# The per-layer gate of a decoder step computed with seven half-size products per pair of token tiles

## The chip, the core and the metric

One Trainium2 chip, one of its cores. TensorE multiplies, VectorE and ScalarE work on rows of SBUF and PSUM, GpSimd issues the gathers and SyncE most of the other transfers. The metric is the device time of one execution in microseconds; lower is better. The kernel before ran three times: 830.54, 834.19 and 836.55 us, with a median of 834.19.

## What is computed

The reference is one layer of a hybrid decoder (retention, gated DeltaNet, a mixture of experts, a per-layer input embedding) over 576 tokens of 1024 numbers, all float32. The change touches the last stage, behind the experts:

```python
h = h + moe
u = rmsnorm(h, norm_ple)
gate = jax.nn.sigmoid(jnp.einsum('bld,de->ble', u, w_ple_gate))   # 1024 x 1024 weights
h = h + gate * jnp.einsum('blp,pd->bld', p_l, w_ple_proj)
# and then the final RMSNorm, which is stored
```

## The kernel before, in words

The 576 tokens lie in five tiles: tiles 0 to 3 have 128 rows, tile 4 has 64. `LAST` is the order in which the last stage takes them (0, 1, 4, 2, 3); k below is a place in that order. Each engine has its own instruction stream, written out by hand in one function per engine, and each runs its stream strictly in the order written. Semaphores tie them together; a wait holds everything behind it on that engine.

The experts run in 12 phases of 128 rows (`down`, L1296). The rows of a phase go from PSUM to `yb` (ScalarE, `y_evac`) and from there to `y_slots` in HBM. GpSimd waits until all phases are stored, then gathers two rows for each token (`ga`, L2706): the first two tiles at once, each later tile when VectorE has used up the buffers of an earlier one.

For each tile, then:
- VectorE `combine` (L2428): two scaled additions of the gathered rows to the residual `h2`; `h3` counts them.
- ScalarE squares the row and takes the root (L1745, L1748), VectorE inverts it (`r3`, L2444).
- TensorE `u3_transpose` (L1398): eight transposes of 128 columns into two PSUM banks; VectorE `u3_evac` (L2438) multiplies by the norm's gain into `u3T`.
- TensorE gate (L1414): for each half of 512 output columns, eight matmuls over the 1024 input columns, in one PSUM bank. The 64-row tile puts its two column quarters side by side on the array (`sides`).
- ScalarE sigmoid (L1759) with the row's factor as its scale, VectorE `gated` (L2451, L2452) times `pp` and plus `h2`; `h4` counts the halves.
- ScalarE squares each half (L1765) and takes the root (`ms_root`, L1769), VectorE `mean0` (L2462) and `finish` (L2470, L2475), and SyncE stores the tile. The last tile is stored in two halves, one scaled by VectorE, one by ScalarE.

`pp`, the product of `p` and `w_proj`, is computed ahead of the gate (`p_product`, L1384): that of tile 0 earlier, those of tiles 1 to 3 before the first transposes, that of tile 4 after them. Sigmoid and Sqrt need different tables on ScalarE; a change of table is an ACT_TABLE_LOAD. `link` marks an instruction of VectorE or ScalarE that the next one must wait for.

The gate's weights are two tiles of 512 output columns, `w_pg[0]` and `w_pg[1]`, 2 MB each, asked for by SyncE at L748 and L750, during the last two phases of the experts. The stored overflow slots (`ov_...`) are a small extra phase.

## Time and profile before

| | us |
|---|---|
| median of three runs | 834.19 |
| the profiled execution's own time | 832.21 |
| span of its instructions | 830.4 |
| busy: TensorE / VectorE / ScalarE / GpSimd | 810.4 / 385.0 / 214.2 / 151.0 |

The span runs from the first instruction to the last; 1.8 us of the execution's own time lie around it. A busy share is an average over stages with different limits: TensorE is busy for 98% of the whole span, and what the change is worth is read from the last 90 us.

### The profile page before, as it was taken

What the parts mean: (1) busy time and instruction counts of PE and PEld (TensorE: products, weight loads), DVE (VectorE), ACT (ScalarE), POOL (GpSimd) and SP (SyncE); (2) the same over time, 40 slices, a digit from 0 to 9 for tenths busy, and PEclk for the clock granted to TensorE, in tenths of its full rate; (3) what the DMA queues carried; (4) which work ended last, traced back from release to release, by engine and by line L of the source; (5) the groups of instructions that cost most, each with busy time, mean ns of one, the idle gap of its engine ahead of it and who ended that gap; (6) DMA issues with size and microseconds to landing.
All of it is one profiled execution on the core that took longest, in us unless ns stands there. A gap on an engine that the chain in (4) does not pass through costs nothing. (4 is left out here: it accounts for less than half of the span.)

```text
span 830.4 us, 12851 instructions
## 1 busy us (share of the span) xinstructions
PE 810.4 (98%) x5194; PEld 509.7 (61%) x5194; DVE 385.0 (46%) x859; ACT 214.2 (26%) x463; POOL 151.0 (18%) x182
## 2 busy tenths in 40 slices
PE   9999999999999999999999999999999999998996
PEld 4545777887889987777777776456343333344452
DVE  3223457584666523664853558636341111106443
ACT  3211152339324311121101101122121111124554
POOL 0234321004055224200220043000100001004000
PEclk9999999999999999999999999999999999999999
DMA  9520354403020200522252024036899999987111
GB/s 359 206 101 9 124 181 152 134 39 109 2 103 3 84 20 13 202 80 94 101 203 87 16 101 176 9 127 252 307 367 399 425 420 415 410 313 221 57 39 51
DMA packets 20896, 135.23 MB, mean 163 GB/s; under 512 B 2420, under 2 KB 3060, under 8 KB 13668
## 3 DMA queue, kind: packets, MB, share of 16 engines
q1 hardware_dynamic: 13392, 103.34, 31.9%
q0 software_dynamic: 4720, 23.83, 8.0%
...
## 5 line engine op out<-in xcount | busy, mean ns | idle before, releaser
L791 PE MATMUL pair<-mem 128*128 128x288 f32 x640 | 158.9, 408 | 0.0
L791 PEld LDWEIGHTS pair<-mem 128*128 128x128 f32 x640 | 120.5, 190 | 35.4 <-ACT mem L1435 2.1
L961 PE MATMUL single<-mem 128*128 128x288 f32 x448 | 110.1, 407 | 0.2
L961 PEld LDWEIGHTS single<-mem 128*128 128x128 f32 x448 | 84.8, 190 | 25.6 <-issue 1.6
L1346 PE MATMUL single<-mem 128*32 128x512 f32 x768 | 85.1, 594 | 0.9 <-DVE mem L2382 0.9
L1435 ACT ACTIVATE mem<-single 128x256 f32<-128x256 f32 (+5 forms) x109 | 44.6, 419 | 126.8 <-PE single L1209 48.5
L1435 ACT ACTIVATE mem<-pair 128x512 f32<-128x512 f32 (+5 forms) x78 | 33.5, 480 | 165.2 <-PE pair L791 63.1
L1414 PE MATMUL pair<-mem 128*128 128x512 f32 (+1 forms) x192 | 63.3, 524 | 0.0
L1346 PEld LDWEIGHTS single<-mem 128*32 128x32 f32 x768 | 23.7, 110 | 52.7 <-issue 51.6
L2375 DVE SCALAR_TENSOR_TENSOR mem<-single,mem 128x256 f32<-128x256 f32 x12 | 5.8, 484 | 102.3 <-PE single L1346 91.1
L1200 PE MATMUL pair<-mem 128*128 128x512 f32 x112 | 51.0, 601 | 0.0
L1414 PEld LDWEIGHTS pair<-mem 128*128 128x128 f32 (+1 forms) x192 | 28.4, 172 | 32.0 <-issue 29.5
L2094 DVE TENSOR_TENSOR mem<-mem,single 128x288 f32<-128x288 f32 x40 | 18.1, 452 | 55.7 <-PE single L961 52.2
L1296 PE MATMUL pair<-mem 128*32 128x512 f32 x384 | 43.7, 595 | 0.0
L1200 PEld LDWEIGHTS pair<-mem 128*128 128x128 f32 x112 | 20.4, 190 | 21.7 <-issue 21.4
L856 PE MATMUL pair<-mem 128*128 128x512 f32 (+1 forms) x96 | 32.1, 526 | 0.0
L2676 POOL DMA_INDIRECT mem<-u_rows,ids x12 | 11.4, 947 | 110.6 <-PE single L1281 100.5
L982 PE MATMUL pair<-mem 128*128 128x288 f32 x112 | 28.4, 409 | 0.2
L832 PE MATMUL pair<-mem 128*128 128x512 f32 x64 | 28.2, 596 | 0.4 <-DVE mem L1806 0.4
L1892 DVE SCALAR_TENSOR_TENSOR mem<-mem,vec 128x512 f32<-128x512 f32 x36 | 27.9, 774 | 1.3
L982 PE MATMUL single<-mem 128*128 128x288 f32 x112 | 27.8, 406 | 0.0
L1296 PEld LDWEIGHTS pair<-mem 128*32 128x32 f32 x384 | 11.3, 110 | 23.1 <-issue 23.0
...
## 6 DMA issues: line engine op xcount, KB each, us to landing
...
y_slots<-mem SPq DMA_DIRECT2D x9, 512.0 KB, 11.2
y_slots<-in_zeros POOLq DMA_DIRECT2D x8, 512.0 KB, 8.5
...
```

Of the source, the lines that this page charges most:

```text
L791: last = nc.tensor.matmul(pb[:, hf, 0:HALF], w(k), rhs[:, k, hf * HALF:(hf + 1) * HALF], start=(k == 0), stop=(k == kk - 1))
L832: last = nc.tensor.matmul(q_bank[t][rows, cols], uT[:, k, t * P:t * P + ntok(t)], ring[0][:, 512 * k + cols.start:512 * k + cols.stop], st ...
L856: last = nc.tensor.matmul(pair[plan.buf[s]][rows, 0, cols], uT[:, k, t * P:t * P + ntok(t)], w[:, k, cols], start=(k == 0), stop=(k == KD ...
L961: last = nc.tensor.matmul(single[plan.buf[s]][:, 0:HALF], lhs[:, k, :], rhs[:, k, :], start=(k == 0 and j in (0, 1, 3, 4)), stop=(k == 3), ...
L982: last = nc.tensor.matmul(fast_bank(s), lhs[:, k, :], rhs[:, k, :], start=(k == 0 and j in (0, 1, 3, 4)), stop=(k == 1), skip_group_check= ...
L1200: last = nc.tensor.matmul(sx_bank[j], rows[:, u, v, :], wgt[:, u, 512 * v:512 * v + 512], start=(i == 0 and j < 5), stop=(i == 3), skip_gr ...
L1296: last = nc.tensor.matmul(pair[p % 2][BS * g:BS * g + BS, n, :], hT[p % 2][:, k, BS * g:BS * g + BS], w_dn[e % 4][:, k, n * 512:(n + 1) * ...
L1346: last = nc.tensor.matmul(single[3][BS * g:BS * g + BS, :], xT[p % 2][:, k, BS * g:BS * g + BS], w_gu[e % 4][:, k, :], start=(k == 0), sto ...
L1414: last = nc.tensor.matmul(pair[(k + 1) % 2][rows, hf, cols], u3T[:, c, t * P:t * P + n], w_pg[hf][:, c, cols], start=(c == 0), stop=(c == ...
L1435: copy = lambda out, in_, scale=1.0: nc.scalar.activation(out, in_, ACT.Copy, scale=scale)
L1892: V.scalar_tensor_tensor(out=acc[m % 2][:, 0:LP], in0=cbuf[m % 2][:, j:j + LP], scalar=conv_w[:, m, j:j + 1], in1=acc[m % 2][:, 0:LP], op0 ...
L2094: V.tensor_tensor(to, plus, single[plan.buf[s]][:, 0:HALF], ALU.add).then_inc(ev(k0), 1)
```

## The change

For a pair of full tiles (0 and 1, then 2 and 3) the gate is a product of 256 x 1024 and 1024 x 1024, cut into 2 x 2 blocks on each side. Before, TensorE computed its eight block products. Now it computes seven, `p1, p2, p5, u2, p3, p4, p7` (L1430), each of four matmuls of 128 x 128 by 128 x 512, on sums and differences of blocks: `t1` to `t4` of the weights (128 x 2048 each, once) and `s1` to `s4` of the transposed rows (128 x 512 each, per pair). VectorE computes all of these. ScalarE copies four results per pair out of PSUM (`keep`), and VectorE adds them to others (`out`, four per pair) before the sigmoid, which now reads SBUF. `LAST` becomes 0, 1, 2, 3, 4, so that the 64-row tile comes last; it keeps its old product (L1466). `pg_sum`, `SUM_AT`, `KEPT` and the like number the sums, copies, squares and roots for the waits.

Besides: `w_pg[1]` is asked for in two halves of 1 MB, the second one only when all expert rows are stored. The last phase's second half is copied by VectorE instead of ScalarE, and one small overflow transpose moves into the middle of that phase. `p_product` of tile 4 moves ahead of the first transposes. The second `combine` step of tile 0 is cut into two halves, so that its first four transposes can begin after the first.

```diff
@@ tables @@
-LAST = [0, 1, 4, 2, 3]
+LAST = [0, 1, 2, 3, 4]
+PG_SUMS = [("t1", 0), ("s1", 0), ("t2", 0), ("s2", 0), ("c11", 0), ("s4", 0), ("s3", 0), ("t4", 0), ("t3", 0), ("c12", 0), ("c21", 0), ("c22", 0),
+   ("s1", 1), ("s2", 1), ("c11", 1), ("s4", 1), ("s3", 1), ("c12", 1), ("c21", 1), ("c22", 1), ("gain", 0), ("gain", 1)]
+SUM_AT = {s: i + 1 for i, s in enumerate(PG_SUMS)}
+PG_ORDER = ["p1", "p2", "p5", "u2", "p3", "p4", "p7"]
+KEPT = {(name, q): 6 + 4 * q + i for q in range(2) for i, name in enumerate(["p1", "p5", "u2", "p4"])}
...
+pg_t1, pg_t2, pg_t4 = (view(at, 4, 512) for at in (OR, BLK + 6144, UT))
+pg_t3 = [view(at, 2, 512) for at in (RINGO + 6144, UT + 3 * D)]
+pg_s1, pg_s2, pg_s4 = ([view(at, 4, P) for at in ats] for ats in
+                       ((RINGO + 4608, BLK + 17408), (RINGO + 5120, BLK + 17920), (RINGO + 5632, RINGO + 8192)))
...
+pg_bank = [(pair[1][:, 0, :], pair[1][:, 1, :], pair[0][:, 0, :]), (pair[0][:, 1, :], pair[1][:, 1, :], pair[0][:, 0, :])]
@@ SyncE @@
-    sp.dma_start(w_pg[1], a["w_pg1"].rearrange("k p c -> p k c")).then_inc(sem("w_pg"), 16)
+    sp.dma_start(w_pg[1][:, 0:4, :], a["w_pg1"][0:4].rearrange("k p c -> p k c")).then_inc(sem("w_pg"), 16)
...
-    sp.wait_ge(sem("h3"), 1)
+    sp.wait_ge(sem("y_stored0"), 16 * ((NPH + 1) // 2))
+    sp.wait_ge(sem("y_stored1"), 16 * (NPH // 2))
     sp.wait_ge(sem("w_pg"), 32)
+    sp.dma_start(w_pg[1][:, 4:8, :], a["w_pg1"][4:8].rearrange("k p c -> p k c")).then_inc(sem("w_pg"), 16)
+    sp.wait_ge(sem("h3"), 2)
+    sp.wait_ge(sem("w_pg"), 48)
@@ TensorE @@
+            if p == NPH - 1 and n == 0:
+                ov_hT(0)
...
-        pe.wait_ge(sem("h3"), k + 1)
+        pe.wait_ge(sem("h3"), k + 2 if k else 1)
         if k >= 2:
             pe.wait_ge(sem("u3T"), 2 * k - 2)
         for c in range(KD):
+            if k == 0 and c == 4:
+                pe.wait_ge(sem("h3"), 2)
             out = single[2 * (k % 2) + c // 4][:, (c % 4) * n:(c % 4 + 1) * n]
             last = nc.tensor.transpose(out, h2[0:n, t, c * P:(c + 1) * P], C("ident")[0:n, 0:n])
         last.then_inc(sem("u3_mm"), 1)
+    p_product(NT - 1)
     u3_transpose(0)
-    p_product(NT - 1)
-    for k, t in enumerate(LAST):
-        n = ntok(t)
-        pe.wait_ge(sem("u3T"), 2 * k + 2)
+    def gate_part(bank, rows, weights, start):
+        for c in range(4):
+            last = nc.tensor.matmul(bank, rows(c), weights(c), start=(start and c == 0), stop=(c == 3), skip_group_check=True)
+        return last
+    for q in range(2):
+        bank_a, bank_b, bank_c = pg_bank[q]
+        first, second = (lambda c: u3T[:, c, 2 * q * P:2 * q * P + P]), (lambda c: u3T[:, c, 2 * q * P + P:2 * q * P + 2 * P])
+        pe.wait_ge(sem("u3T"), 4 * q + 1)
         pe.wait_ge(sem("w_pg"), 32)
...
+        pe.wait_ge(sem("pp"), 4 + q)
+        gate_part(bank_a, first, lambda c: w_pg[0][:, c, :], True).then_inc(sem("pg_mm"), 1)
+        u3_transpose(2 * q + 1)
+        pe.wait_ge(sem("u3T"), 4 * q + 2)
+        if q:
+            pe.wait_ge(sem("pp"), KEPT["p4", 0])
+        gate_part(bank_b, lambda c: first(c + 4), lambda c: w_pg[0][:, c + 4, :], True).then_inc(sem("pg_mm"), 1)
+        pe.wait_ge(sem("pp"), 5)
+        pe.wait_ge(sem("pg_sum"), SUM_AT["s1", q])
+        gate_part(bank_c, lambda c: pg_s1[q][:, c, :], lambda c: pg_t1[:, c, :], True).then_inc(sem("pg_mm"), 1)
+        pe.wait_ge(sem("pp"), KEPT["p1", q])
+        pe.wait_ge(sem("pg_sum"), max(SUM_AT["t2", 0], SUM_AT["s2", q]))
+        gate_part(bank_a, lambda c: pg_s2[q][:, c, :], lambda c: pg_t2[:, c, :], False).then_inc(sem("pg_mm"), 1)
+        u3_transpose(2 * q + 2)
+        pe.wait_ge(sem("pp"), KEPT["p5", q])
+        pe.wait_ge(sem("pg_sum"), SUM_AT["s4", q])
+        gate_part(bank_c, lambda c: pg_s4[q][:, c, :], lambda c: w_pg[1][:, c + 4, :], False).then_inc(sem("pg_mm"), 1)
+        pe.wait_ge(sem("pg_sum"), max(SUM_AT["t4", 0], SUM_AT["c11", q]))
+        gate_part(bank_b, lambda c: second(c + 4), lambda c: pg_t4[:, c, :], True).then_inc(sem("pg_mm"), 1)
+        pe.wait_ge(sem("pp"), KEPT["u2", q])
+        pe.wait_ge(sem("pg_sum"), max(SUM_AT["t3", 0], SUM_AT["s3", q]))
+        gate_part(bank_a, second, lambda c: pg_t3[c // 2][:, c % 2, :], False).then_inc(sem("pg_mm"), 1)
+    pe.wait_ge(sem("u3T"), 2 * NT)
+    for hf in range(2):
+        if hf:
+            pe.wait_ge(sem("pp"), KEPT["p4", 1])
+        for c in range(KD):
+            for rows, cols in sides(4):
+                last = nc.tensor.matmul(pair[1][rows, hf, cols], u3T[:, c, 4 * P:TOK], w_pg[hf][:, c, cols],
+                                        start=(c == 0), stop=(c == KD - 1))
+        last.then_inc(sem("pg_mm"), 1)
@@ ScalarE @@
-        copy(yb[b][:, 512:D], pair[b][:, 1, :]).then_inc(sem("y_ready"), 1)
+        if e_done < NPH:
+            copy(yb[b][:, 512:D], pair[b][:, 1, :]).then_inc(sem("y_ready"), 1)
...
+    def gate(k, hf):
+        t, n = LAST[k], ntok(LAST[k])
         act.wait_ge(sem("r3"), k + 1)
+        if k < 4:
+            act.wait_ge(sem("pg_sum"), SUM_AT[("c11", "c12", "c21", "c22")[2 * (k % 2) + hf], k // 2])
+            half = sgp[k % 2][:, 512 * hf:512 * hf + 512]
+            last = nc.scalar.activation(half, half, ACT.Sigmoid, scale=ms[:, 2, t:t + 1])
+        else:
+            act.wait_ge(sem("pg_mm"), 15 + hf)
+            act.wait_ge(sem("h4"), 5 + hf)
             for rows, cols in sides(t):
+                last = nc.scalar.activation(sgp[0][0:n, 512 * hf + cols.start:512 * hf + cols.stop], pair[1][rows, hf, cols],
                                             ACT.Sigmoid, scale=ms[0:n, 2, t:t + 1])
+        last.then_inc(sem("sgp"), 1)
...
+    def keep(name, q):
+        act.wait_ge(sem("pg_mm"), 7 * q + PG_ORDER.index(name) + 1)
+        k, hf, bank = {"p1": (0, 0, 0), "u2": (0, 1, 0), "p4": (1, 0, 1), "p5": (1, 1, 2)}[name]
+        if q:
+            act.wait_ge(sem("h4"), 2 * k + hf + 1)
+        copy(sgp[k][:, 512 * hf:512 * hf + 512], pg_bank[q][bank]).then_inc(sem("pp"), 1)
+    row_root(0)
+    row_root(1)
+    keep("p1", 0)
+    gate(0, 0)
+    keep("p5", 0)
+    half_square(0, 0)
+    keep("u2", 0)
+    row_root(2)
+    gate(0, 1)
+    keep("p4", 0)
+    half_square(0, 1)
+    last_root(0)
...
+    half_square(2, 1)
+    last_root(2)
+    keep("p4", 1)
+    gate(3, 0)
+    half_square(3, 0)
+    gate(3, 1)
+    link(nc.scalar.activation(hT[0][0:1, 0, 0:1], C("eps", 1), ACT.Sqrt))
+    half_square(3, 1)
+    last_root(3)
+    gate(4, 0)
+    half_square(4, 0)
+    gate(4, 1)
+    link(nc.scalar.activation(hT[0][0:1, 0, 0:1], C("eps", 1), ACT.Sqrt))
+    half_square(4, 1)
+    last_root(4)
@@ VectorE @@
+    dve.wait_ge(sem("dn_mm"), NPH)
+    dve.wait_ge(sem("y_stored1"), 16 * ((NPH - 1) // 2))
+    V.tensor_copy(yb[1][:, 512:D], pair[1][:, 1, :]).then_inc(sem("y_ready"), 1)
...
+    w11, w12, w22 = w_pg[0][:, 0:4, :], w_pg[1][:, 0:4, :], w_pg[1][:, 4:8, :]
+    def weights_1():
+        dve.wait_ge(sem("w_pg"), 32)
+        V.tensor_tensor(pg_t1, w12, w11, ALU.subtract).then_inc(sem("pg_sum"), 1)
+    def weights_2():
+        dve.wait_ge(sem("w_pg"), 48)
+        dve.wait_ge(sem("pg_sum"), SUM_AT["t1", 0])
+        V.tensor_tensor(pg_t2, w22, pg_t1, ALU.subtract).then_inc(sem("pg_sum"), 1)
+    def weights_4():
+        dve.wait_ge(sem("pg_sum"), SUM_AT["t2", 0])
+        V.tensor_tensor(pg_t4, w_pg[0][:, 4:8, :], pg_t2, ALU.subtract).then_inc(sem("pg_sum"), 1)
+    def weights_3():
+        dve.wait_ge(sem("pp"), 5)
+        V.tensor_tensor(pg_t3[0], w22[:, 0:2, :], w12[:, 0:2, :], ALU.subtract)
+        V.tensor_tensor(pg_t3[1], w22[:, 2:4, :], w12[:, 2:4, :], ALU.subtract).then_inc(sem("pg_sum"), 1)
+    def rows(q, second, half):
+        return u3T[:, 4 * half:4 * half + 4, 2 * q * P + P * second:2 * q * P + P * second + P]
+    def rows_1(q):
+        dve.wait_ge(sem("u3T"), 4 * q + 4)
+        V.tensor_tensor(pg_s1[q], rows(q, 1, 0), rows(q, 1, 1), ALU.add).then_inc(sem("pg_sum"), 1)
+    def rows_2(q):
+        dve.wait_ge(sem("pg_sum"), SUM_AT["s1", q])
+        V.tensor_tensor(pg_s2[q], pg_s1[q], rows(q, 0, 0), ALU.subtract).then_inc(sem("pg_sum"), 1)
+    def rows_4_3(q):
+        dve.wait_ge(sem("pg_sum"), SUM_AT["s2", q])
+        V.tensor_tensor(pg_s4[q], rows(q, 0, 1), pg_s2[q], ALU.subtract).then_inc(sem("pg_sum"), 1)
+        V.tensor_tensor(rows(q, 1, 0), rows(q, 0, 0), rows(q, 1, 0), ALU.subtract).then_inc(sem("pg_sum"), 1)
+    def out(name, q):
+        after, k, hf, kept, bank = {"c11": ("p2", 0, 0, "p1", 1), "c12": ("p3", 0, 1, "u2", 2),
+                                    "c21": ("p7", 1, 0, "p4", 0), "c22": ("p7", 1, 1, "p5", 0)}[name]
+        h = sgp[k][:, 512 * hf:512 * hf + 512]
+        dve.wait_ge(sem("pg_mm"), 7 * q + PG_ORDER.index(after) + 1)
+        dve.wait_ge(sem("pp"), KEPT[kept, q])
+        V.tensor_tensor(h, pg_bank[q][bank], h, ALU.add).then_inc(sem("pg_sum"), 1)
+    weights_1()
     combine(0)
     u3_evac(0)
     combine(1)
     r3(0)
+    u3_evac(1)
+    rows_1(0)
+    weights_2()
+    rows_2(0)
+    r3(1)
+    out("c11", 0)
+    rows_4_3(0)
+    weights_4()
+    gated(0, 0)
     combine(2)
-    r3(1)
+    weights_3()
+    u3_evac(2)
+    r3(2)
+    out("c12", 0)
     combine(3)
-    u3_evac(1)
-    r3(2)
+    gated(0, 1)
+    mean0(0)
+    finish(0)
+    out("c21", 0)
+    out("c22", 0)
+    r3(3)
+    gated(1, 0)
+    u3_evac(3)
+    rows_1(1)
+    rows_2(1)
+    gated(1, 1)
+    mean0(1)
+    out("c11", 1)
+    rows_4_3(1)
+    finish(1)
     combine(4)
-    r3(3)
+    gated(2, 0)
+    u3_evac(4)
     r3(4)
-    for k in range(NT):
-        if 1 <= k < NT - 1:
-            u3_evac(k + 1)
-        for hf in range(2):
-            gated(k, hf)
-            if hf == 0:
-                mean0(k)
-        finish(k)
+    out("c12", 1)
+    gated(2, 1)
+    mean0(2)
+    finish(2)
+    out("c21", 1)
+    out("c22", 1)
+    gated(3, 0)
+    gated(3, 1)
+    mean0(3)
+    finish(3)
+    gated(4, 0)
+    mean0(4)
+    gated(4, 1)
+    finish(4)
@@ GpSimd @@
-            pool.wait_ge(sem("h3"), k - 1)
+            pool.wait_ge(sem("h3"), k)
```

VectorE in the first pair, before: from the second tile's `combine` to its `u3_evac`.

```order
L2428 SCALAR_TENSOR_TENSOR mem<-mem,wcomb 128x1024 [waits ga01]
L2428 SCALAR_TENSOR_TENSOR mem<-mem,wcomb 128x1024 [waits ga11,dve_link]
L2444 RECIPROCAL ms<-ms 128x1 [waits ms_root]
L2428 SCALAR_TENSOR_TENSOR mem<-mem,wcomb 64x1024 [waits ga00]
L2428 SCALAR_TENSOR_TENSOR mem<-mem,wcomb 64x1024 [waits ga10,dve_link]
L2444 RECIPROCAL ms<-ms 128x1 [waits ms_root]
L2428 SCALAR_TENSOR_TENSOR mem<-mem,wcomb 128x1024 [waits ga01]
L2428 SCALAR_TENSOR_TENSOR mem<-mem,wcomb 128x1024 [waits ga11,dve_link]
L2438 TENSOR_TENSOR mem<-single,vec 128x4x128 [waits u3_mm]
```

Four tiles are combined ahead of the second tile's scaling. VectorE now, from the first row sum `s1` (L2626) to the third tile's `combine` (L2540); L2607 and L2612 are `t2` and `t4`, L2646 is `c11`, L2564 and L2565 are `gated`:

```order
L2626 TENSOR_TENSOR mem<-mem 128x512 [waits u3T]
L2607 TENSOR_TENSOR mem<-mem 128x2048 [waits pg_sum,w_pg]
L2631 TENSOR_TENSOR mem<-mem 128x512 [waits pg_sum]
L2557 RECIPROCAL ms<-ms 128x1 [waits ms_root]
L2646 TENSOR_TENSOR mem<-pair,mem 128x512 [waits pp,pg_mm]
L2636 TENSOR_TENSOR mem<-mem 128x512 [waits pg_sum]
L2637 TENSOR_TENSOR mem<-mem 128x4x128
L2612 TENSOR_TENSOR mem<-mem 128x2048 [waits pg_sum]
L2564 TENSOR_TENSOR mem<-mem 128x512 [waits sgp]
L2565 TENSOR_TENSOR mem<-mem 128x512 [waits dve_link]
L2540 SCALAR_TENSOR_TENSOR mem<-mem,wcomb 128x1024 [waits ga00]
L2540 SCALAR_TENSOR_TENSOR mem<-mem,wcomb 128x1024 [waits ga10,dve_link]
```

The third tile's `combine` stood right behind the second's; now ten operations of the first pair stand ahead of it, and TensorE's third set of transposes waits for it.

ScalarE at the end of the program, before: both sigmoids (L1759) and squares (L1765) of the last tile.

```order
L1759 ACT_TABLE_LOAD [waits h4,pg_mm]
L1759 ACTIVATE mem<-pair,ms 128x512 [waits r3]
L1765 ACTIVATE mem,rs<-mem 128x512 [waits h4]
L1759 ACTIVATE mem<-pair,ms 128x512 [waits h4,pg_mm]
L1763 ACT_TABLE_LOAD
```

And now, where L1809 is the sigmoid of the fourth tile (it waits for the sums `c21` and `c22`), L1814 that of the last, L1821 a square and L1828 a root:

```order
L1809 ACT_TABLE_LOAD [waits pg_sum]
L1809 ACTIVATE mem<-mem,ms 128x512 [waits r3]
L1821 ACTIVATE mem,rs<-mem 128x512 [waits h4]
L1809 ACTIVATE mem<-mem,ms 128x512 [waits pg_sum,r3]
L1870 ACT_TABLE_LOAD
L1870 ACTIVATE mem<-const 1x1
L1821 ACTIVATE mem,rs<-mem 128x512 [waits h4,act_link]
L1828 ACTIVATE ms<-rs 128x1 [waits mean0,ms]
L1814 ACT_TABLE_LOAD [waits h4,pg_mm]
L1814 ACTIVATE mem<-pair,ms 64x256 [waits r3]
```

Both sigmoids of the fourth tile now stand behind the pair's last product, and those of the last tile behind them.

## Rows read from the trace of the kernel before

**Rows 1.** The chain of waits, in order of time (start us, us, what).
```profile
739.44 5.97 DMA y_slots<-mem
...
747.48 5.20 DMA mem<-y_slots,posu
...
752.77 1.29 DVE mem L2428
...
755.20 1.88 PE pair L1384 x16
757.08 7.06 PE pair L1414 x16
764.14 0.87 PE single L1398 x8
765.01 13.73 PE pair L1414 x32
...
779.39 10.67 PE pair L1414 x48
...
802.62 20.62 PE pair L1414 x48
```

**Rows 2.** TensorE by time (start us, us, form, count, idle before).
```profile
740.53 10.57 PE L1384 MATMUL pair<-mem 128*128 128x512 f32 x24 [0.68 <-issue]
754.11 1.09 PE L1398 MATMUL single<-const,mem 128*128 128x128 f32 x8 [3.01 <-DVE mem L2428]
```

**Rows 3.** Stretches: busy us of each engine, granted clock, DMA share, GB/s.
```profile
core 0: us, PE busy (x) PEld busy (x) DVE busy (x) ACT busy (x) POOL busy (x), PEclk, DMA share, GB/s
700.00:740.00 40.00, 39.53 (x411) 14.05 (x403) 4.76 (x10) 7.51 (x17) 0.00 (x0) 1.00 1.01 401
...
751.00:757.00 6.00, 2.99 (x25) 1.92 (x24) 3.77 (x5) 2.51 (x3) 1.80 (x2) 1.00 0.84 259
757.00:790.00 33.00, 33.00 (x115) 15.63 (x113) 19.18 (x29) 17.71 (x33) 5.24 (x4) 1.00 0.34 99
790.00:823.00 33.00, 33.00 (x114) 15.98 (x112) 14.71 (x24) 16.16 (x27) 0.00 (x0) 1.00 0.12 41
```

**Rows 4.** DMA issues from 736 us on (count, KB, us to landing).
```profile
out_y<-mem SPq DMA_DIRECT2D x3, 512.0 KB, 2.6
```

**Rows 5.** The transfers that SyncE issues, by time.
```profile
728.45 0.38 SPq L750 DMA_DIRECT2D mem<-in_w_pg  x1
```

**Rows 6.** Groups of instructions on VectorE, shapes apart (busy us, mean ns, idle before).
```profile
L2173 DVE TENSOR_TENSOR mem<-mem 128x2048 f32<-128x2048 f32 x4 | 9.0, 2278 | 0.0
...
L2451 DVE TENSOR_TENSOR mem<-mem 128x512 f32<-128x512 f32 x8 | 5.5, 691 | 12.7 <-ACT mem L1759 12.7
```

**Rows 7.** VectorE by time.
```profile
756.44 2.60 DVE L2428 SCALAR_TENSOR_TENSOR mem<-mem,wcomb 128x1024 f32<-128x1024 f32 x2
...
783.22 1.28 DVE L2475 SCALAR_TENSOR_TENSOR mem<-mem,ms 128x1024 f32<-128x1024 f32 x1
784.42 0.75 DVE L2438 TENSOR_TENSOR mem<-single,vec 128x256 f32<-128x256 f32 x2
```

**Rows 8.** ScalarE by time: a 64-row sigmoid, and the program's end.
```profile
792.95 0.95 ACT L1759 ACTIVATE mem<-pair,ms 64x256 f32<-64x256 f32 x2
...
823.26 0.69 ACT L1759 ACTIVATE mem<-pair,ms 128x512 f32<-128x512 f32 x1 [2.65 <-PE pair L1414]
823.97 1.28 ACT L1763 ACT_TABLE_LOAD   x1
825.26 0.20 ACT L1763 ACTIVATE mem<-const 1x1 f32<-1x1 f32 x1
825.50 0.63 ACT L1765 ACTIVATE mem<-mem 128x512 f32<-128x512 f32 x1
826.03 0.19 ACT L1765 ACTIVATION_READ_ACCUMULATOR mem<-mem 128x1 f32 x1
826.25 0.29 ACT L1769 ACTIVATE ms<-rs 128x1 f32<-128x1 f32 x1
826.77 0.72 ACT L1435 ACTIVATE mem<-mem,ms 128x512 f32<-128x512 f32 x1 [0.23 <-DVE ms L2470]
```

90 lines of the change are left out of this document (46 added, 44 removed).

## The prediction

> **What bounds the kernel now.** First the chain of waits, for what the end hangs on [rows 1]. From 757.08 us to 823.2 it is TensorE's gate without a gap: 64 matmuls of 128x512, the two halves of the 64-row tile and four sets of transposes. Each matmul leaves two records, so 13.73 us for 32 records are 0.858 us per matmul; a set of transposes takes 0.87 to 1.09 us (I take 0.95; 0.68 for the 64-row tile), and half of the 64-row tile 10.67 - 8 x 0.858 = 3.8 us. Ahead of the gate the chain is made of transfers: the last expert store (5.97 us), a gather (5.20 us), VectorE's `combine`, transposes, the small product of tile 4. Next TensorE by time [rows 2]: it finished the products of tiles 1 to 3 at 751.1 and idled 3.01 us for the first `combine`. Then the busy time by stretch [rows 3]: beside a TensorE that is 100% busy, VectorE works 19.2 of 33 us, then 14.7 of 33; ScalarE 17.7 and 16.2. There is room, but it has to be in the right places. Last, the end of ScalarE's stream [rows 8]: from the last gate matmul at 823.24 to the last scaling at 827.49 it is 4.25 us, then a store; the span ends at 830.4, 2.9 us behind.
>
> **The start of the gate.** The overflow's small transpose moves under the last expert phase, and two copies go side by side, so TensorE's products of tiles 1 to 3 should begin 0.4 us earlier (740.1 for 740.53) and end at 750.65; the idle behind them [rows 2] now takes the 1.88 us of tile 4's product [rows 1], to 752.5. Four transposes (0.5) need the first half of the second `combine` step: its gather landed about 752.7, the addition's half takes 0.69. To be in time it has to land at 751.8. Its way begins with the expert store. With 1 MB of gate weights less in front (asked for at 728.45, [rows 5]), at the 401 GB/s of [rows 3] 2.6 us of traffic, the store should land 2.3 us sooner. Bounds: only its earlier issue, 0.4; or the whole way down to an undisturbed 512 KB store, 2.6 us for 5.97 [rows 1, 4], 3.8 in all. I take the middle, as some of the traffic ahead of it stays. The late quarter then runs beside the first gathers: between 0 and 2.6 us of delay for them, I take 0.6. So the gather lands 1.7 us earlier, 751.0, and does not matter: TensorE sets the start. Transposes to 753.55, half of the scaling (0.69), first product at **754.3**, 2.8 us earlier than the 757.08 of before. With the bad bounds (0.4 sooner, 1.5 of delay) it is 756.2. The late quarter itself has until `t2` at 760.7, over 17 us: no cost.
>
> **TensorE's own work.** Per pair 28 matmuls instead of 32: 8 x 0.858 = **6.9 us** less for both. The start and this together would give 9.7 us, if nothing else waited. Both further terms come from what VectorE gets.
>
> **VectorE's added work.** From [rows 6]: a sum of 128x2048 takes 2.28 us, one of 128x512 0.69; back to back an operation hides 0.07 of itself behind the next (783.22 to 784.42 for 1.28, [rows 7]). `t1` runs before the gathers land, at no cost: VectorE is idle there; if the first weight half landed after 746 it would push `combine`. The rest, `t2`, `t4`, `t3` (7.0 us), eight row sums (5.5) and eight output sums (5.5), is 18 us on top of the 37.7 of the stretches in [rows 3]. The eight copies on ScalarE, a sigmoid's 0.69 each at most [rows 8], fall into its waits; if those went they would cost 5.5 us. Its table loads grow from eleven to fifteen, 5.1 us more [rows 8]; in the middle they fall into its waits too, at the end they are in the walk below.
> - First pair: `p1` 754.3 to 757.7, transposes to 758.7, second tile scaled by 760.0. Then in this order on VectorE: `s1` 0.7, `t2` 2.2, `s2` 0.6, reciprocal 0.1, `c11` 0.6, `s4`, `s3` 1.2, `t4` 2.2, `gated` 1.4, `combine` of the third tile 2.6 (as in [rows 7]): 11.6 us, done at 771.6. TensorE is through `p2`, `p5`, `u2` (3 x 3.43) at 769.0, and its next instruction is the transposes of that third tile. **It stalls 2.7 us.** Then transposes 0.95 and three products 10.3: 782.9.
> - Second pair: 24.0 of matmuls, 0.95 and 0.68 of transposes, and again a stall, for the 64-row tile's `combine`, which stands behind `finish` of the second tile: 1.4 us. It ends at **809.9**; the 64-row tile takes 7.6 more, to 817.5. TensorE is done 5.7 us earlier than before.
>
> **The end.** It no longer hangs on TensorE. Both halves of the fourth tile are complete only with `p7`, at 809.9, and four sigmoids, four squares and two roots stand behind it on ScalarE, each waiting for VectorE and back. By [rows 6 to 8]: VectorE is in `finish` of the third tile to 812.2 (its root came late, as the fifth tile's square and root stand ahead of it on ScalarE); `c21` to 812.95; table load 1.28, sigmoid 0.69, `gated` 1.45, square with its read 0.73, second sigmoid 0.69, load 1.28, the dummy 0.20, square 0.73, root 0.29 with small gaps: 820.2. Load 1.28, sigmoid of the 64-row half 0.95, `gated` 1.45, square 0.73, sigmoid 0.95, load 1.28, dummy 0.20, square 0.73, root 0.29, reciprocal 0.16, last scaling 0.72, 0.3 of gaps: **828.9**. That is 19 us behind the last full product, where before 4.25 us lay behind the last one, and 1.4 us later than 827.49.
>
> **The sum.** Start -2.8, matmuls -6.9, tile 4's transposes and halves the same, stalls +2.7 and +1.4, and 11.4 us instead of 4.25 behind TensorE's end, +7.15: together +1.5; by the clock times +1.4. Against the profiled execution's 832.21 that is 833.6; the median of the three runs stands 2.0 above it, and the same step from there gives 835.6. With runs that lie 6 us apart (830.54 to 836.55) I take the middle, 834.4. About 1%, 8.3 us, is what a measurement of this kernel can tell from no change.
>
> **A rule weighed.** TensorE idled 3.01 us before the gate, and the granted clock stayed 1.00 in that stretch and in the next [rows 2, 3]. The stall that I expect before the third transposes is 2.7 us, a little shorter, so I leave the clock at its upper level. The Trainium skill, "TensorE: Matmul & The Clock Gate", section "Why this matters for your kernels", warns that an idle gap between bursts of matmuls can send the clock to half. By that rule the sum would be the 838 to 840 of the second rival below; by the rows nothing is added.
>
> **The rivals.**
> - **The sums stay hidden (20%).** If VectorE's added operations cost the path nothing, the first stall goes and `c21` starts at once: the same walk with those operations at zero ends at 822.7, 4.8 us before 827.49, so 827.4 to 829.4 by the two bases. For it: VectorE idles 33 of the 66 us. Against it: the ten operations ahead of the third `combine` are written in a row, and each has a price in the trace. In parts (shorter sums, a `finish` that gets out of the way) it gives anything down to there.
> - **The clock falls at the stall (12%), slower.** Place: the idle ahead of the third tile's transposes. The trace shows an idle of 3.01 us that left the clock alone, so I let it decide only beyond that, if VectorE is 0.4 us later than I have it. Price: with the transposes and `p3` at half, 4.4 us on TensorE and as much at the end, 838 to 840; with the pair's three products at half 10.1, 844 to 846.
> - **The start doesn't come earlier (8%).** The late quarter delays the gathers or VectorE is held, the gate starts at 756.2 or later: +2 us on the forecast, 836.4.
> - That seven products aren't what runs can be left out: the order shows 28 matmuls of 128x512 per pair.
>
> **How the numbers follow.** The forecast (end of the chain from 0.5 us earlier to 3.5 us later than before) has 60%, the rivals 20, 12 and 8. The faster end of the first rival less the scatter of medians is 827 to 829; the milder clock case and its scatter reach 840. I leave out the worst clock case and the far tail of the first rival: 829 to 840. Faster by over 1% needs more than 8.3 of the 9.7 us of start and matmuls, and no new wait: 4%. Slower by over 1% needs the clock's worst case or two bad bounds together: 7%. Within 1%: 89%.
>
> **What the profile of the changed kernel would show.** The first product near 754.3; the expert store landing near 743; TensorE idle 2 to 3 us once, before the third set of transposes, released by VectorE's `combine`, and about 1 us before the fifth; granted clock 1.00 in both pairs. TensorE's last matmul near 817.5, and a chain of waits whose last 15 us and more go back and forth between ScalarE and VectorE. If TensorE is without a stall and the chain runs through it to within 8 us of the end, my account of VectorE is wrong; if the clock row shows less than 1.00 after the stall, the second rival holds; if the gate starts later than 755.5, the transfers were misjudged.

## The result, and the profile after

| | before | changed | ratio, 95% interval |
|---|---|---|---|
| median, same chip, 6 runs each | 834.38 us | 839.96 us | 1.008 [1.0058, 1.0102] |
| profiled execution | 832.21 us | 835.63 us | |
| its span | 830.4 us | 833.8 us | |
| busy: TensorE / VectorE / ScalarE | 810.4 / 385.0 / 214.2 | 803.8 / 404.1 / 223.5 | |

The changed kernel is 5.6 us slower: less than 1% (8.3 us), but the interval lies well clear of no change. The single times lie between 835.63 and 842.95, and the profiled execution is the fastest of them. So there are two questions: why is even this execution 3.4 us slower than the profiled one of before, where I forecast +1.4, and why are the others slower still? In one run below, cover_fill, one of its 12 times is 1058.72 us, at a granted clock of 0.751: this slow execution counts in the run's median (836.76 us without it) and not in its ratio.

TensorE by time in the changed kernel, from the overflow phase on (start us, us, form, count, idle before). L1405 are the small products of `p_product`, L1421 the transposes, L1430 the gate products, L1466 the 64-row tile.

```profile
738.99 1.05 PE L1351 MATMUL single<-mem 128*32 128x256 f32 x16
740.94 12.45 PE L1405 MATMUL pair<-mem 128*128 128x512 f32 x40 [0.91 <-issue]
753.32 1.09 PE L1421 MATMUL single<-const,mem 128*128 128x128 f32 x8
755.20 3.70 PE L1430 MATMUL pair<-mem 128*128 128x512 f32 x8 [0.79 <-DVE mem L2551]
...
772.59 1.09 PE L1421 MATMUL single<-const,mem 128*128 128x128 f32 x8 [2.52 <-DVE mem L2540]
773.52 13.90 PE L1430 MATMUL pair<-mem 128*128 128x512 f32 x32
...
800.19 0.71 PE L1421 MATMUL single<-const,mem 64*128 64x64 f32 x8 [1.24 <-DVE mem L2540]
800.83 10.57 PE L1430 MATMUL pair<-mem 128*128 128x512 f32 x24
811.33 7.13 PE L1466 MATMUL pair<-mem 128*64 128x256 f32 x64
```

This answers to [rows 1, 2]. The products of tile 4 are now among the 40 records at 740.94, the gate's first product starts at 755.20 instead of 757.08, and the idle of 3.01 us ahead of the first transposes is gone. In its place stand a stall of 2.52 us ahead of the third tile's transposes and one of 1.24 us ahead of the 64-row tile's, both released by VectorE's `combine` (L2540). TensorE ends at 818.46, 4.8 us before 823.2.

The same kernel's stretches (busy us of each engine, granted clock, DMA share, GB/s), answering to [rows 3]:

```profile
769.00:773.00 4.00, 1.48 (x7) 0.60 (x6) 3.93 (x5) 1.64 (x4) 0.20 (x1) 1.00 0.00 0
...
819.00:831.00 12.00, 0.00 (x0) 0.00 (x0) 7.77 (x14) 9.70 (x19) 0.00 (x0) 0.63 0.11 44
```

In the stall VectorE is busy for 3.93 of 4 us, and in this execution the granted clock stays at 1.00. In the last 12 us TensorE has nothing to do, and the granted clock falls there, where it costs nothing. What runs there is ScalarE's stream, to be read against [rows 8] (start us, us, form, count, idle before):

```profile
819.10 1.28 ACT L1870 ACT_TABLE_LOAD   x1
...
821.69 1.28 ACT L1814 ACT_TABLE_LOAD   x1
822.99 0.95 ACT L1814 ACTIVATE mem<-pair,ms 64x256 f32<-64x256 f32 x2
825.41 0.63 ACT L1821 ACTIVATE mem<-mem 64x512 f32<-64x512 f32 x1 [1.47 <-DVE mem L2565]
...
827.13 1.28 ACT L1876 ACT_TABLE_LOAD   x1
...
829.93 0.72 ACT L1485 ACTIVATE mem<-mem,ms 64x512 f32<-64x512 f32 x1 [0.22 <-DVE ms L2583]
```

The last scaling ends at 830.65, 12.2 us behind TensorE; before it was 4.25 us behind.

### The profile page after: what moved, and what is told of

The parts are those of the page before. It is cut to its first block and busy times, and to the rows that moved or that the text cites. A ratio compares the mean times of both kernels' runs of the same rounds, so it can differ in the third digit from the quotient of the medians.

```text
span 833.8 us, 12879 instructions
## 1 busy us (share of the span) xinstructions
PE 803.8 (96%) x5178; PEld 506.3 (61%) x5178; DVE 404.1 (48%) x882; ACT 223.5 (27%) x475; POOL 150.4 (18%) x182
## 5 line engine op out<-in xcount | busy, mean ns | idle before, releaser
L811 PEld LDWEIGHTS pair<-mem 128*128 128x128 f32 x640 | 120.3, 190 | 35.6 <-ACT mem L1485 2.1
L1485 ACT ACTIVATE mem<-pair 128x512 f32<-128x512 f32 (+5 forms) x85 | 37.7, 488 | 162.7 <-PE pair L811 63.1
L1220 PE MATMUL pair<-mem 128*128 128x512 f32 x112 | 51.0, 601 | 0.0
L1430 PE MATMUL pair<-mem 128*128 128x512 f32 x112 | 49.3, 595 | 0.9 <-DVE mem L2551 0.8
L1430 PEld LDWEIGHTS pair<-mem 128*128 128x128 f32 x112 | 20.8, 190 | 25.9 <-issue 23.9
L1220 PEld LDWEIGHTS pair<-mem 128*128 128x128 f32 x112 | 20.3, 190 | 21.7 <-issue 21.4
L876 PE MATMUL pair<-mem 128*128 128x512 f32 (+1 forms) x96 | 32.1, 525 | 0.0
L2874 POOL DMA_INDIRECT mem<-u_rows,ids x12 | 11.4, 948 | 110.6 <-PE single L1301 100.7
L852 PE MATMUL pair<-mem 128*128 128x512 f32 x64 | 28.5, 601 | 0.4 <-DVE mem L1914 0.4
L1743 ACT ACTIVATE mem<-single,mem 128x256 f32<-128x256 f32 x12 | 5.7, 476 | 74.3 <-PE single L1368 74.3
```

The costliest lines, as they stand in the source:

```text
L811: last = nc.tensor.matmul(pb[:, hf, 0:HALF], w(k), rhs[:, k, hf * HALF:(hf + 1) * HALF], start=(k == 0), stop=(k == kk - 1))
L852: last = nc.tensor.matmul(q_bank[t][rows, cols], uT[:, k, t * P:t * P + ntok(t)], ring[0][:, 512 * k + cols.start:512 * k + cols.stop], st ...
L876: last = nc.tensor.matmul(pair[plan.buf[s]][rows, 0, cols], uT[:, k, t * P:t * P + ntok(t)], w[:, k, cols], start=(k == 0), stop=(k == KD ...
L1220: last = nc.tensor.matmul(sx_bank[j], rows[:, u, v, :], wgt[:, u, 512 * v:512 * v + 512], start=(i == 0 and j < 5), stop=(i == 3), skip_gr ...
L1430: last = nc.tensor.matmul(bank, rows(c), weights(c), start=(start and c == 0), stop=(c == 3), skip_group_check=True)
L1485: copy = lambda out, in_, scale=1.0: nc.scalar.activation(out, in_, ACT.Copy, scale=scale)
```

## The experiments

Each kernel was timed against the kernel before on its own chip in five rounds, in three batches (medians of before 833.95, 833.25, 833.85) and a last one (833.80). The table puts the profiles side by side. "Gate" is the start of the first L1430 product; "to the end" is from there to the end of ScalarE's last scaling. "None" stands where two products that are put ahead of the branch leave no idle.

| kernel | ratio [95%] | median us | idle behind the branch | gate | to the end |
|---|---|---|---|---|---|
| before | 1 | 833.8 | 0.68 | 757.1 | 70.4 |
| start_only | 0.9983 [0.9966, 0.9999] | 832.22 | 0.94 | 755.0 | 70.5 |
| changed, first profile | 1.008 [1.0058, 1.0102] | 839.96 | 0.91 | 755.2 | 75.45 |
| again | 1.0073 [1.0056, 1.0091] | 839.94 | 2.94 | 760.5 | 77.15 |
| quarter_undone | 1.0073 [1.005, 1.0095] | 839.65 | 0.96 | 757.7 | 77.2 |
| fill | 1.0067 [1.0043, 1.0091] | 838.15 | 0.94 | 754.6 | 75.5 |
| cover | 1.0062 [1.0042, 1.0082] | 838.34 | 0.66 | 756.4 | 77.0 |
| cover_fill | 1.0036 [1.002, 1.0053] | 836.82 | 0.82 | 756.4 | 75.5 |
| combine_early | 1.0041 [1.0022, 1.0059] | 836.47 | 2.25 | 760.3 | 74.8 |
| combines_cover | 1.0028 [1.0016, 1.004] | 835.80 | none | 758.2 | 74.2 |
| before_cover | 0.9981 [0.9968, 0.9993] | 832.09 | none | 757.0 | 70.4 |
| reordered | 0.9936 [0.9913, 0.9959] | 828.41 | 2.69 | 760.7 | 65.3 |
| reordered_cover | 0.9921 [0.99, 0.9942] | 826.61 | 0.96 | 756.9 | 65.3 |

**again.** The changed kernel unchanged, for a second profile.

> The changed kernel itself once more. Its profiled execution took 835.63 us at a mean granted clock of 0.993; five others took 837.8 to 843.0 us at 0.989 to 0.991. The clock theory: TensorE's clock falls to its lower level in the stall ahead of the third transposes, but not in every execution, and only the profiled one escaped. Then this profile shows, in most cases, a stretch below 1.00 behind that stall, the span is some 838 us or more, and the median is 838 to 842. The chain theory: the length is VectorE's and ScalarE's waits alone, and the clock differs only because TensorE ends earlier. Then the granted clock is 1.00 in the whole gate in slow executions too.

The profile caught an execution of 842.6 us, and that was worth more than the median. TensorE by time:

```profile
740.80 1.05 PE L1351 MATMUL single<-mem 128*32 128x256 f32 x16
744.78 13.89 PE L1405 MATMUL pair<-mem 128*128 128x512 f32 x40 [2.94 <-issue]
...
777.87 1.46 PE L1421 MATMUL single<-const,mem 128*128 128x128 f32 x8 [2.51 <-DVE mem L2540]
779.13 15.26 PE L1430 MATMUL pair<-mem 128*128 128x512 f32 x32
```

And its stretches, with the granted clock:

```profile
740.00:753.00 13.00, 10.06 (x44) 4.35 (x37) 3.87 (x3) 2.00 (x3) 3.77 (x4) 0.87 0.69 255
772.00:780.00 8.00, 5.49 (x18) 2.75 (x17) 7.93 (x8) 4.49 (x8) 1.65 (x1) 0.90 0.00 0
780.00:787.00 7.00, 7.00 (x16) 3.09 (x15) 4.19 (x7) 2.60 (x4) 0.90 (x1) 0.87 0.27 75
```

The span is 7.0 us longer than in the first profile (the clean one, as the clock does not fall in it), and the rows account for all of it. 1.8 lie ahead of the overflow phase (740.80 for 738.99). 2.0 are a longer idle behind that phase's branch (2.94 for 0.91, "issue": the engine waits for nothing that the profile shows). 1.4 are the products behind it, which run at a granted clock of half at first (13.89 for 12.45). 1.7 are the transposes and products behind the VectorE stall, at half as well (1.46 and 15.26 for 1.09 and 13.90; the stall itself is the same, 2.51). So the clock does fall at the stall, in this execution and not in the first one, and it falls at a second place that I had not looked at.

The mean granted clock of the executions without a profile says how common that is. It is 0.993 in the first profile, with no fall before TensorE's end, and 0.989 in this one, with two. Of the twelve executions of the changed kernel, eight stand at 0.989 or 0.990 and took 839.88 to 842.95 us; the four at 0.991 to 0.993 took 835.63 to 838.95.

The 1.8 us ahead of the overflow phase are there almost from the start. TensorE's first 48 products of 128x512, in the first profile and in this one:

```profile
5.63 21.21 PE L852 MATMUL pair<-mem 128*128 128x512 f32 x48 [0.40 <-DVE mem L1914]
5.76 23.18 PE L852 MATMUL pair<-mem 128*128 128x512 f32 x48 [0.53 <-DVE mem L1914]
```

They take 20.9 to 21.5 us in ten of the profiles and 23.2 to 23.5 in four (again, combine_early, combines_cover, reordered). I call these four the late executions. The trace has the reason: the granted clock rises to 1.00 at 10.45 us here and at 6.37 in the first profile (4.6 to 6.9 us in the ten, 10.4 to 11.0 in the four), while TensorE starts at 1.45 in all. The 48 products start at 5.76 us, so 4.7 us of them at half cost 2.3, and 23.18 is 2.3 more than the shortest, 20.87. The mean clock above leaves this out, as it counts only what follows the rise.

**start_only.** Everything of the change but the seven products and their sums.

```diff
-            sp.dma_start(w_pg[1], a["w_pg1"]...)
+            sp.dma_start(w_pg[1][:, 0:4, :], a["w_pg1"][0:4]...)
...
-            u3_transpose(0)
             p_product(NT - 1)
+            u3_transpose(0)
...  (copies, the overflow transpose and the cut combine as in the change; eight products and LAST as before)
```

> The kernel before with only the change's start: the last quarter of the gate's weights asked for when the rows are stored, the small overflow transpose and the split copy, the small product of tile 4 ahead of the first transposes, the first combine in two halves. All 64 matmuls, the old order of tiles. As TensorE is the chain through the whole gate, the 2.8 us that the gate starts earlier should reach the end: 831 to 832 us against 834.4. If the transfers take the gain back, no difference.

The gate starts at 754.97 and runs without a gap (70.5 us to the end, as before), and the median falls by 0.17%, some 1.5 us (the interval ends at 0.9999). This part of the change is a small gain. The whole loss, some 7.7 us by the medians, comes with the seven products and their sums. The profiled executions are 2.0 us apart (830.17 and 832.21), so the median gains nearly what the profile gains.

**quarter_undone.** The second half of `w_pg[1]` asked for with the first again.

```diff
-            sp.dma_start(w_pg[1][:, 0:4, :], a["w_pg1"][0:4]...)
+            sp.dma_start(w_pg[1], a["w_pg1"]...)
...
-            sp.dma_start(w_pg[1][:, 4:8, :], a["w_pg1"][4:8]...)
```

> The changed kernel with the gate's second weight tile asked for whole (2 MB) where its first half is asked for now. The last expert store then lands about 2.4 us later, at 745.9 in the changed kernel's time, the first combine's second step at 753.4 to 754 instead of 752.0, and the gate starts 1 us later or a little more, as the transposes wait for it. The store theory: 0.5 to 1.5 us slower than the changed kernel, 840.5 to 841.5. The rival: the stalls behind take the difference up, or the gathers gain what the store loses: 839 to 840.5, no difference.

The median can't be told from the changed kernel's, but the profile shows what the late request buys. The expert store lands 2.3 us later (745.8 for 743.5), and the first transposes wait for `combine`:

```profile
755.62 1.32 PE L1417 MATMUL single<-const,mem 128*128 128x128 f32 x8 [2.18 <-DVE mem L2536]
```

The gate starts at 757.72 instead of 755.20, and the clock falls behind this idle (0.83 in the stretch from 755 to 765 us; the first product's records take 5.40 us for 3.70 and the transposes ahead of them 1.32 for 1.09, so this fall cost 1.9 us). At the stall of 2.52 us ahead of the third transposes it does not. Why the median shows no loss is not settled; the spreads (837.0 to 840.94 and 838.43 to 842.6) allow a microsecond either way.

**fill.** Three products of 128x512 into a bank that nobody reads ahead of the third tile's transposes, one ahead of the 64-row tile's.

```diff
+                for _ in range(3 if q == 0 else 1):
+                    nc.tensor.matmul(single[0][:, :], C("ones"), w_pg[0][:, 0, :], start=True, stop=True)
                 u3_transpose(2 * q + 2)
```

> The changed kernel with four idle-filling matmuls of 128x512 into a free PSUM bank: three ahead of the third transposes (2.6 us in a stall of 2.5), one ahead of the fifth (0.86 in 1.2). Their result is not used. The clock theory: TensorE no longer idles, the clock stays up in all executions (0.992 or more) and the median drops to 834.5 to 836.5, about 4 us under the changed kernel. The chain theory: the waits stay as they are, so the median stays at 839 to 841.

The stall is filled (products from 769.34 to 772.08, transposes at 772.02), and the gate takes 75.5 us, exactly as in the clean profile of the changed kernel: the transposes come no later. But single times still reach 842.36, four of the six at a mean clock of 0.989 to 0.991, and the gain in the median, 1.8 us, is inside the intervals. Alone it settled nothing.

**combine_early.** VectorE does `combine` of the third tile ahead of `t4` and the first `gated`.

```diff
+            combine(2)
             weights_4()
             gated(0, 0)
-            combine(2)
```

> The changed kernel with VectorE's combine of the third tile ahead of the weight difference t4 and of gated. By the walk through the streams TensorE's stall of 2.5 us ahead of the third transposes goes, about 2 us of idle appear later, ahead of the second pair's third product, and the end comes 0.4 us earlier. The clock theory: if the shorter idle leaves the clock alone, 834.5 to 836.5 us and a mean clock of 0.992 or more; if it does not, 838 or more. The chain theory: 839 to 841 as before, minus 0.4.

TensorE by time:

```profile
744.38 14.14 PE L1405 MATMUL pair<-mem 128*128 128x512 f32 x40 [2.25 <-issue]
...
775.04 1.04 PE L1421 MATMUL single<-const,mem 128*128 128x128 f32 x8
775.91 13.90 PE L1430 MATMUL pair<-mem 128*128 128x512 f32 x32
...
796.35 7.11 PE L1430 MATMUL pair<-mem 128*128 128x512 f32 x16 [2.23 <-DVE mem L2626]
804.69 0.71 PE L1421 MATMUL single<-const,mem 64*128 64x64 f32 x8 [1.24 <-DVE mem L2540]
```

The stall ahead of the third transposes is gone, but 2.23 us stand ahead of the second pair's third product instead, released by one of the row sums that VectorE now reaches later. Moving one instruction moves the wait. In the profiles only 0.6 us of the gate's length is gained (74.8 for 75.45), while the median is 3.5 us better. The clock does not fall at either remaining stall of this profile; that the rest of the gain is the falls at the third transposes, which are gone with the stall, fits but is not shown. Two of its 11 executions still stand at a mean clock of 0.988 and 0.989.

**before_look.** The kernel before once more, for the place where its own clock may fall.

> The kernel before once more, for one more profile of it. Its 22 other executions show mean clocks from 0.993 to 0.999 and 831.7 to 836.1 us. If this one lies under 0.998, its trace shows where the clock falls in it: at the idle ahead of the gate, or at the branch behind the overflow phase.

It came out at 832.16 us with a granted clock of 0.999, and shows no fall.

**cover.** Two products (1.7 us, unused) ahead of the overflow phase's branch.

```diff
             ov_down(0)
+            for _ in range(2):
+                nc.tensor.matmul(single[3][:, :], C("ones"), w_proj[:, 0, 0:512], start=True, stop=True)
```

> The changed kernel with two matmuls of 128x512 (1.7 us, their result not used) behind the overflow's last matmuls, where TensorE idled 0.9 us in one profile of the changed kernel and 2.9 us in another, whose clock fell there. The branch theory: the idle is the fetch of the code behind the branch, which goes on beside the matmuls, and the clock's fall there costs about 2 us; covered, the clock stays up, the mean is 0.991 or more in most executions, and the median is 837.5 to 839 against 840. The rival: the fetch begins only when TensorE has come to the branch; then idle and matmuls add up, and the median is 841 or more.

The single times draw together, 837.29 to 839.06, and the products behind the branch run at full clock (12.44 us). The stall ahead of the third transposes is still there, and at it the clock falls:

```profile
742.11 12.44 PE L1407 MATMUL pair<-mem 128*128 128x512 f32 x40 [0.66 <-issue]
...
773.76 1.97 PE L1423 MATMUL single<-const,mem 128*128 128x128 f32 x8 [2.52 <-DVE mem L2542]
```

**cover_fill.** Both at once.

> The changed kernel with both idles of TensorE covered: two products (1.7 us, into a bank nobody reads) behind the overflow phase's down product, ahead of the branch, and three ahead of the transposes for the third tile (one ahead of the 64-row tile's). The extra results are unused, so the output is that of the changed kernel. Theory A (what the changed kernel loses beyond 835.6 us is TensorE's clock falling at these two idles, and neither cover alone removed both): the granted clock is 0.99 or more by the records but with no stretch at half in the gate or behind the branch, and the median is 835 to 837 us, ratio about 1.003, with single times within 2.5 us of each other. Rival B (the clock falls have another cause, as the start of the kernel or the phases ahead of 700 us): 838 to 840 us, ratio 1.006 as with either cover alone, and stretches at half that stand elsewhere or stay where they were.

The median is 836.82, ratio 1.0036: 3.1 us less than the changed kernel, where each half alone gave 1.6 to 1.8. The profile:

```profile
742.15 12.45 PE L1407 MATMUL pair<-mem 128*128 128x512 f32 x40 [0.82 <-issue]
...
771.12 2.74 PE L1454 MATMUL single<-mem,const 128*128 128x512 f32 x6
773.80 1.09 PE L1423 MATMUL single<-const,mem 128*128 128x128 f32 x8
774.73 13.90 PE L1432 MATMUL pair<-mem 128*128 128x512 f32 x32
```

No stretch at half is left before TensorE's end. The idle ahead of the branch's products hardly shrinks for the two products: from the start of L1351's matmuls to the product behind the branch it is 3.8 us (738.38 to 742.15), where the first profile has 1.95 and again has 3.98. So either the two products cost 1.8 us themselves, or this is a long idle that they partly fill; no run tells these apart. Either way, with these 1.8 us off the median stands at 835.0, and it was 835.63 that the clean first profile had. I take that as an estimate of what the change's mechanism costs without the clock and the long idle; it assumes that the other executions have the 1.8 us too.

**before_cover.** The same two products in the kernel before.

> The kernel before with the same two products (1.7 us, into a bank nobody reads) behind the overflow phase's down product, ahead of the branch. Its times come in two groups, about 832 us at a granted clock of 0.998 and more and about 835 us at 0.993 to 0.995. Theory A (the idle behind the branch is where its clock falls too, in about half of its executions): the group at 835 us is gone, all times lie within 2.5 us of each other, at 832 to 834 us (the two products can delay the gate by up to 1.5 us), the granted clock is 0.996 or more in all, ratio 0.997 to 1.001. Rival B (the kernel before loses its clock elsewhere, for one at the 3.0 us ahead of its first transposes): both groups stay, moved together by 0 to 1.5 us, median 834 to 835.5 us, ratio 1.000 to 1.003.

832.09 us, ratio 0.9981, with 11 of 12 times in 831.1 to 833.31 (one at 836.31). So the kernel before also loses some 1.7 us that the cover takes away. TensorE by time:

```profile
754.07 1.09 PE L1400 MATMUL single<-const,mem 128*128 128x128 f32 x8 [1.96 <-DVE mem L2430]
```

This kernel still idles 1.96 us for `combine` (3.01 in [rows 2]), so up to 3 us of lateness behind the branch can be absorbed there: with two products more its gate still starts at 757.0. The change has put tile 4's product into that idle. It has nothing left to absorb a late TensorE with. That the clock falls in some executions of the kernel before is inferred; no profile of it caught one. Its mean clock fits: in the first batch the nine executions above 834.7 us stand at 0.993 to 0.997, the eight below 832.5 at 0.997 to 0.999, and with the cover all twelve at 0.997 or more. The amounts do not close: a long idle and a fall together (2.0 and 1.7 us) would exceed the 3.01 us by 0.7, and the cover takes 1.7.

**combines_cover.** The cover, `combine(2)` early, and `combine(4)` ahead of `finish(1)`.

```diff
+            combine(2)
             weights_4()
             gated(0, 0)
-            combine(2)
...
-            finish(1)
             combine(4)
+            finish(1)
```

> The changed kernel with the two products ahead of the branch, combine(2) ahead of weights_4 and gated(0, 0), and combine(4) ahead of finish(1) on VectorE: both of its late combine steps early, nothing else reordered. Theory A (TensorE's end sets the end, by the ScalarE and VectorE work that is left behind the last product, so a microsecond taken out of TensorE's stalls comes off the end): against the 836.82 us of the kernel with both idles covered by extra products, TensorE ends 1.5 to 3 us earlier and the time is 834 to 835.5 us, ratio 1.000 to 1.002. Rival B (VectorE and ScalarE are themselves the bound from the third tile on, so TensorE's earlier end only lengthens the work behind it): TensorE ends earlier but the time is 836 to 838 us, ratio 1.003 to 1.005.

Between the theories. The median, 835.80 us, lies 0.3 above A's range and 0.2 below B's. The profile leans to A: from the start of the gate TensorE takes 61.3 us instead of 63.3, and the whole 74.2 instead of 75.5, so of 2.0 us taken out of TensorE 1.25 arrive at the end, and the rest becomes chain behind it (12.9 us for 12.2). The median is 1.0 us better than cover_fill's.

**reordered.** The changed kernel's instructions, all of them, in another order on VectorE and ScalarE. VectorE's list from the third `combine` on, changed kernel (-) and reordered (+):

```diff
-combine(2); weights_3(); u3_evac(2); r3(2); out("c12", 0); combine(3); gated(0, 1); mean0(0); finish(0)
-out("c21", 0); out("c22", 0); r3(3); gated(1, 0); u3_evac(3); rows_1(1); rows_2(1); gated(1, 1); mean0(1)
-out("c11", 1); rows_4_3(1); finish(1); combine(4); gated(2, 0); u3_evac(4); r3(4); out("c12", 1)
-gated(2, 1); mean0(2); finish(2); out("c21", 1); out("c22", 1); gated(3, 0); gated(3, 1)
...
+combine(2); rows_4_3(0); gated(0, 0); combine(3); u3_evac(2); weights_3(); out("c12", 0); out("c21", 0)
+r3(1); mean0(0); r3(2); combine(4); gated(0, 1); u3_evac(3); out("c22", 0); rows_1(1); gated(1, 0)
+rows_2(1); gated(1, 1); rows_4_3(1); out("c11", 1); finish(0); gated(2, 0); out("c12", 1); u3_evac(4)
+mean0(1); mean0(2); finish(1); r3(3); r3(4); gated(2, 1); out("c21", 1); out("c22", 1); gated(3, 0); gated(3, 1)
...
```

The sums and `combine` steps that TensorE waits for go ahead; `mean0` and `finish`, for which in the end only stores wait, go behind them, and so do the reciprocals `r3`, for which the sigmoids wait. On ScalarE the copies and sigmoids go ahead of the squares and roots (`half_square`, `last_root`).

> The changed kernel with the same instructions on every engine, in another order on VectorE and ScalarE alone: the weight differences t2 and t4 between the first tiles' work, the combines of the later tiles early, the finishes late, both sigmoids of a tile next to each other before a change of table. By the walk through the streams TensorE has no stall of over 1 us left and ends about 4 us earlier, and the end of ScalarE's stream comes 9.8 us earlier than in the changed kernel's walk. The order theory (the change lost its gain to the waits between VectorE and ScalarE): 828 to 831 us, against some 840, and under the kernel before. The clock theory alone (the clock falls whatever the order, as the small idles at the start remain): the stalls' 4 us and no more, 835 to 837. If neither, 839 or more.

828.41 us, ratio 0.9936 [0.9913, 0.9959]: 11.5 us less than the changed kernel and 4.8 less than before, with the same arithmetic. The gate has no stall, TensorE takes 58.85 us of it, and ScalarE ends 6.5 us behind. This profile is a late execution and has the long idle behind the branch, 2.69 us, with products of 14.13 us behind it.

**reordered_cover.** The same with the two products ahead of the branch.

> The reordered kernel (the changed kernel's instructions in another order on VectorE and ScalarE, which has no stall in the gate) with the same two products ahead of the overflow phase's branch; their results are unused. Its only idle long enough to matter was the 2.7 us behind the branch. Theory A (the idle behind the branch lets the clock fall and costs some 2 us in part of the executions): 826 to 827.5 us, ratio 0.991 to 0.992. Rival B (the fall costs nothing there, since what follows waits for VectorE anyway, or the two products delay the gate by what they save): 828 to 830 us, ratio 0.994 to 0.996.

826.61 us, 825.73 to 827.47, ratio 0.9921: the lowest median of all, though 1.8 us below reordered's with intervals of the ratio that overlap. TensorE by time from the gate on, and ScalarE's end:

```profile
756.86 3.70 PE L1430 MATMUL pair<-mem 128*128 128x512 f32 x8 [0.83 <-DVE mem L2551]
760.40 1.04 PE L1421 MATMUL single<-const,mem 128*128 128x128 f32 x8
761.27 10.46 PE L1430 MATMUL pair<-mem 128*128 128x512 f32 x24
771.57 1.04 PE L1421 MATMUL single<-const,mem 128*128 128x128 f32 x8
772.45 13.90 PE L1430 MATMUL pair<-mem 128*128 128x512 f32 x32
...
797.45 0.71 PE L1421 MATMUL single<-const,mem 64*128 64x64 f32 x8
798.09 10.57 PE L1430 MATMUL pair<-mem 128*128 128x512 f32 x24
808.58 7.13 PE L1466 MATMUL pair<-mem 128*64 128x256 f32 x64
```

```profile
814.22 1.28 ACT L1814 ACT_TABLE_LOAD   x1
815.52 1.94 ACT L1814 ACTIVATE mem<-pair,ms 64x256 f32<-64x256 f32 x4
817.94 0.63 ACT L1821 ACTIVATE mem<-mem 64x512 f32<-64x512 f32 x1 [0.48 <-DVE mem L2565]
...
821.48 0.72 ACT L1485 ACTIVATE mem<-mem,ms 64x512 f32<-64x512 f32 x1 [0.22 <-DVE ms L2583]
```

One group follows the other without a wait, and both sigmoids of the 64-row tile go back to back behind one table load, where the changed kernel waited 1.47 us between them.

## Why the prediction was right or wrong

The forecast was 834.4 us, practically no change; the kernel is 5.6 us slower. The direction was that of the sum (+1.4), the size was not.

- **The start of the gate: right in mechanism, 0.9 us too early.** 755.20 for 754.3. The store landed at 743.5 (predicted near 743) and the gather did not bind. 0.6 us lay in the execution itself, which was late by that much from 305 us on; the rest is an idle behind the branch of 0.91 us where I took the 0.68 of before. The store itself came 2.3 us sooner by the later request (743.5 against quarter_undone's 745.8), the 2.3 that I had, although the middle of my bounds of 0.4 and 3.8 is 2.1.
- **TensorE's own work: right.** From the first product to its last, TensorE takes 63.26 us; I had 63.2.
- **VectorE's added work: right.** Stalls of 2.52 and 1.24 us at the two places named, for 2.7 and 1.4. The rival in which the sums stay hidden is refuted.
- **The end: right in mechanism, 0.8 us short.** ScalarE ends 12.2 us behind TensorE, where I had 11.4. About half of this is a slip of addition: the terms that I wrote down behind `c21` add up to 16.4 us (7.3 and 9.0), not to the 15.95 from 812.95 to 828.9, and the profile has 16.4 (814.22 to 830.65). With the right sum the forecast would have been 0.4 us higher. The rest is `c21`, done at 814.2 for 812.95, as VectorE's `finish` of the third tile ended later than I had it. The store behind it all took 3.15 us instead of 2.9.
- **The sum.** For the clean execution: +1.4, and 0.9, 0.8 and 0.3 on top, make +3.4, which is what the two profiled executions are apart (835.63 and 832.21). Here sizes were wrong, not a step.
- **The rule weighed: this step failed.** "... the granted clock stayed 1.00 ... so I leave the clock at its upper level." One idle of 3.01 us in one execution was taken for a rule. Over the profiles, the stall of 2.5 us left the clock alone in two (the first of the changed kernel, quarter_undone) and brought it to half in two (again, cover), at a price of 1.5 to 1.7 us. The Trainium skill, "TensorE: Matmul & The Clock Gate", section "Why this matters for your kernels", had the warning, for gaps somewhat longer than this stall, and the traces agree with it in part of the executions, down to this length. My rival for this had the right place, a chance that was too small (12%) and a price that was too high (4.4 us). That its 838 to 840 us hold the measured 839.96 is luck: one fall at that price stood in for 2.0 us that the sum was short, a smaller fall and what happens at the branch.
- **What no step had: the branch.** The idle behind the overflow phase's branch stood in [rows 2] with 0.68 us, and I did not ask whether it varies. It is 0.7 to 1.0 us in most profiles and 2.25 to 2.94 in three (again, combine_early, reordered). In all three the clock fell there too, so it costs up to 2.0 + 1.7 us. In the kernel before, the idle ahead of the first transposes can take up to 3 us of that; the change used it up. I counted that idle as free room for tile 4's product ("takes the 1.88 us") and did not name what it could cover. How much this costs in the median is not shown: start_only has used up the same idle, and its median gains only 0.3 us less than its profile (1.7 and 2.0), with an interval of some 1.4 us either way.
- **The median, an estimate.** Covering both idles takes 3.1 us from the changed kernel, and 1.8 more stand in what is left, so the clock and the long idle cost it about 4.9 in the median; covering the branch takes 1.7 from the kernel before. The difference is 3.2. With the 2.9 to 3.4 of the mechanism (835.0 against 832.09 with covers, or the two profiled executions) that makes 6.1 to 6.6, against 5.6 and 6.0 measured. So the loss is about half mechanism and half clock and branch; how the second half divides between the stall and the branch no run shows.
- **Open.** Why the idle behind the branch has two lengths. In the twelve profiles that have one it ends 1.4 us after a 16 KB packet on the queue of instruction fetches has arrived, long or short (739.5 and 740.94 in the first profile, 743.4 and 744.78 in again); in before_cover and combines_cover, which have none, the packet arrived 2.5 and 2.2 us ahead. That points to code that has to be loaded; no run removed that load. The packet starts 0.5 to 0.8 us ahead of L1351's matmuls where the idle is short, and 0.8 to 1.5 us behind them in again, combine_early and reordered. It is as late in cover, cover_fill and reordered_cover (1.1 to 1.4 us), which are not late executions, so there the two products may delay the load or fill a long idle. All three long idles stand in late executions (at the same instruction 307.3 to 307.8 us for 304.9 to 305.5); why the clock rises later in these, and whether it has to do with the branch, stays open.
